# Hybrid attention/S5/MoE layer: hand-placed buffers, early loads, GLU in fp32r, eight-slot q/k store ring

## Chip, core and metric

One core of one Trainium2 chip runs the kernel in one launch, fp32 in and out. The metric is device microseconds of that core.

## What is computed

One layer over 2048 tokens of width 1024. The parts before the residual, cut to what matters:

```python
h = rmsnorm(x, norm_attn)
q, k, v, u = split(h @ w_in)                      # 4 x 512 columns
# differential attention: 4 heads, two causal softmax maps each, ALiBi
a = softmax(q1 k1^T + bias) - lam * softmax(q2 k2^T + bias);  o = a @ v     # then RMSNorm
# S5: 32 groups of 16 channels, each drives a 64-dim complex diagonal state
y = gelu(Re(C states) + D u)
y = y * sigmoid(y @ w_glu + b_glu);  ssm = rmsnorm(y, ssm_norm)
x = x + concat([attn, ssm]) @ w_out
x = x + hier_moe(rmsnorm(x))                      # 32 experts, top 2 of one group
return rmsnorm(x, norm_final)
```

## The kernel before

Every stage is a function with a block of its own: each engine has its instruction list written out by hand, with semaphores between them. A stage ends with a clearing of its semaphores and a barrier of all engines, so nothing of the next stage starts before the last engine of this one is done, the waits for its DMA stores included. Buffers of a stage are allocated at its start and freed at its end.

**norm_project_prepare** (from line 116). Tile by tile of 128 tokens, it normalizes x, transposes it into two fp32r parts (`ht`, hi and lo), and multiplies by w_in in three products (hi hi, lo hi, hi lo). 32 units give v and u. The transposed parts are also stored in `hT_d`. From 225 us on 32 further units, numbered P1 = 32 to 63, give q and k by columns: unit n is a head's 128 columns of q or k for a block of 512 tokens, 8 blocks k of 3 matmuls. Their slices come back from `hT_d` into a ring of 12. ACT writes the hi part of a unit (`hi_out`, L371), DVE the lo part (`lo_out`, L453), ACT's queue stores both (`parts_store`, L379) from `ev`, which has four slots, so two pairs. Before `hi_out` writes a pair it waits until the store of the unit two before has landed. In the same time DVE makes the S5 parameters of eight batches of four groups (`matrices_w`, `matrices_q`, `levels`), two with the tiles, six with the q/k units: `matrices_w(b)` follows lo_out of unit `w_at_unit(b)`, four units apart. PE transposes its result two units later (`batch`, L702, L707). POOL stores q, w and the tables of each batch to DRAM. SP loads u back as `U` and, when all is done, stores the taps.

**s5_groups** (from 774). 16 pairs of groups. SP first loads w, tables (cos, sin), the taps as a Toeplitz block `M`, which DVE has cleared before, and q for the first four groups, then the rest. Per pair: ACT regroups U, PE transposes (L912), ACT copies (`u_group`, L898), PE makes the inputs (L927), DVE turns and adds them (L861 to L864) and scans twice (L871), POOL turns back (L843, L845), PE makes the outputs (L946 to L948), ACT does the GELU into U. States of pair p+2 are queued on PE behind the outputs of pair p.

**s5_gate** (from 962). PE transposes U by 16 columns of 4 blocks, and ACT copies each from PSUM into `yT` (L996), writing every eighth element, 32 bytes apart. Then 16 units n (t = n // 4 a block of 512 tokens, oc = n % 4) of 4 fp32 matmuls (L1052), which run as 8 passes; ACT takes the sigmoid (L1003), DVE the product (L1016), its square (L1020) and the scaled result (L1021). For each t PE adds up the squares of 4 channel blocks and 128 tokens with one-column products (L1043); 16 of them in the program are 32 in the trace. SP stores `ssmT` for each t. At the end DVE and ACT make the root and the reciprocal, `srs`.

**attention** (from 1060). 64 units u (4 heads, 16 row tiles). SP loads q and k of block 0, then five small parameters, v, then blocks 1 to 3. POOL and DVE make the ALiBi ramp (L1148, L1156, L1150). DVE runs score(0), `lam()` (27 tiny steps), score(1), and so on; scores need q, k and the ramp. `out_projection` and the expert stage follow.

## Time and profile before

| | us |
|---|---|
| median of 3 runs | 2337.03 (2335.39 to 2339.47) |
| the profiled execution | 2335.25 |
| its span in the profile | 2333.7 |
| PE busy | 2061.0 (88%) |
| DVE busy | 1365.5 (59%) |
| ACT busy | 1070.4 (46%) |
| POOL busy | 517.3 (22%) |

The profile is one execution. Times in it count from the start of the span. Matmuls are pipelined, so PE can be shown busy while it is slowed by its clock; the granted clock of a stretch is a share of 2.4 GHz, and it has two levels, 2.4 and 1.2 GHz. A releaser is what ended an engine's idle time.

### The profile page before, as it was taken

The page shows a single profiled execution, that of the slowest core. Times are in us where ns is not written, and L with a number is a line of the kernel's source. Part 1 is how long each engine was busy: PE and PEld are TensorE (multiplying, and loading weights), DVE is VectorE, ACT ScalarE, POOL GpSimd, SP SyncE. Part 2 cuts the span into 40 slices and gives each one's busy share as a digit, 9 for nine tenths or more (in the row PEclk, how much of TensorE's full clock was granted, in tenths as well). Part 3 has the DMA queues.
Part 4 walks back from the last instruction along what each step waited for, and adds up shares of the span by engine and source line. Part 5 has one row for each costly group of instructions (what it writes and reads, how often), then busy time and mean ns, then how long its engine had stood idle before and what let it go on. Part 6 is the DMA issues. An engine that isn't in the chain of part 4 may idle for free. (4 is left out here: it accounts for less than half of the span.)

```text
span 2333.7 us, 32329 instructions
## 1 busy us (share of the span) xinstructions
PE 2061.0 (88%) x10318; PEld 1695.1 (73%) x10319; DVE 1365.5 (59%) x2364; ACT 1070.4 (46%) x1580; POOL 517.3 (22%) x631
## 2 busy tenths in 40 slices
PE   6999999698969889897999569999999999999980
PEld 5888777585558677775888358888888888888860
DVE  4674567262357778684444677476658856354544
ACT  3332111134147777774222336475557756454443
POOL 2000011041000000000000025454445644344440
PEclk9999999799879999998999679999999999999995
DMA  8676865650183331203443459698869979576737
GB/s 250 206 233 209 295 234 197 181 199 20 64 206 82 75 91 37 64 1 116 139 141 122 163 221 322 215 340 313 275 231 356 394 245 358 164 261 185 264 82 305
DMA packets 170682, 458.38 MB, mean 196 GB/s; under 512 B 20497, under 2 KB 69729, under 8 KB 144993
## 3 DMA queue, kind: packets, MB, share of 16 engines
q1 hardware_dynamic: 123616, 285.43, 35.8%
q0 software_dynamic: 30848, 138.24, 19.4%
q10 hardware_dynamic: 16128, 33.56, 4.1%
q8 instruction: 51, 0.84, 0.2%
q14 instruction: 39, 0.31, 0.0%
HBM read 342.08 MB, written 115.10 MB: 196 GB/s over the span
## 5 line engine op out<-in xcount | busy, mean ns | idle before, releaser
L1950 DVE TENSOR_TENSOR w_down_lo<-w_down_raw,w_down_hi 128x2048 fp32r<-128x2048 f32 x64 | 144.1, 2289 | 123.2 <-ACT w_down_hi L1887 123.2
L1182 DVE CUSTOM_DVE_ANT_0 scores<-c_bank,alibi 128x512 f32<-128x512 f32 (+3 forms) x320 | 176.3, 606 | 39.2 <-PE c_bank L1295 39.1
L1321 PE MATMUL c_bank<-v_head,map_T 128*128 128x128 f32 x1088 | 150.8, 284 | 32.3 <-ACT map_T L1237 31.0
L1321 PEld LDWEIGHTS c_bank<-v_head,map_T 128*128 128x128 f32 x1088 | 134.0, 194 | 44.6 <-ACT map_T L1237 44.0
L2034 PE MATMUL m_bank<-w_down_hi,hidden_T_hi 128*128 128x512 f32 x392 | 159.7, 407 | 6.8 <-DVE w_down_lo L1950 6.8
L1950 DVE TENSOR_TENSOR w_gate_lo<-w_gate_raw,w_gate_hi 128x2048 fp32r<-128x2048 f32 x63 | 141.6, 2288 | 35.2 <-ACT w_gate_hi L1887 34.1
L1228 ACT ACTIVATE scores<-scores,neg_max 128x128 f32<-128x128 f32 (+15 forms) x128 | 153.5, 1199 | 17.6 <-DVE neg_max L1186 17.6
L2013 PE MATMUL m_bank<-w_gate_hi,rows_T_hi 128*128 128x512 f32 x392 | 156.2, 399 | 4.0 <-issue 2.6
L2013 PE MATMUL m_bank<-w_up_hi,rows_T_hi 128*128 128x512 f32 x392 | 159.0, 406 | 0.0
L2035 PE MATMUL m_bank<-w_down_lo,hidden_T_hi 128*128 128x512 f32 x392 | 155.9, 398 | 0.0
L2014 PE MATMUL m_bank<-w_gate_lo,rows_T_hi 128*128 128x512 f32 x392 | 155.8, 398 | 0.0
L2015 PE MATMUL m_bank<-w_gate_hi,rows_T_lo 128*128 128x512 f32 x392 | 155.7, 397 | 0.0
L1950 DVE TENSOR_TENSOR w_up_lo<-w_up_raw,w_up_hi 128x2048 fp32r<-128x2048 f32 x64 | 146.1, 2286 | 16.3 <-ACT w_up_hi L1887 16.3
L2015 PE MATMUL m_bank<-w_up_hi,rows_T_lo 128*128 128x512 f32 x392 | 154.8, 395 | 0.0
L2014 PE MATMUL m_bank<-w_up_lo,rows_T_hi 128*128 128x512 f32 x392 | 154.8, 395 | 0.0
L1294 PE MATMUL c_bank<-k_hi,q_parts 128*128 128x512 f32 (+3 forms) x320 | 125.9, 398 | 23.6 <-DMA k_lo<-kT_d 14.0
L1606 POOL IOTA count_i<- 128x128 int32 x1 | 0.2, 235 | 656.5 <-POOLq L63 656.5
L1887 ACT ACTIVATE w_up_hi<-w_up_raw 128x2048 fp32r<-128x2048 f32 x62 | 118.6, 1914 | 0.0
L1887 ACT ACTIVATE w_down_hi<-w_down_raw 128x2048 fp32r<-128x2048 f32 x62 | 115.5, 1906 | 6.4 <-DMA w_down_raw<-in_w_down_dram 6.4
L1891 ACT ACTIVATE rows_T_hi<-m_bank 128x512 fp32r<-128x512 f32 x100 | 54.5, 596 | 138.9 <-PE m_bank L2006 138.9
L1295 PE MATMUL c_bank<-k_lo,q_parts 128*128 128x512 f32 (+3 forms) x320 | 116.1, 369 | 0.0
L1902 ACT ACTIVATE rows_out<-m_bank,slot_gate 128x512 f32<-128x512 f32 x98 | 67.5, 688 | 105.9 <-PE m_bank L2039 105.9
(400 smaller groups left out, 5154.0 us busy)
## 6 DMA issues: line engine op xcount, KB each, us to landing
w_gate_raw<-in_w_gate_dram SPq DMA_DIRECT2D x64, 1024.0 KB, 8.2
w_up_raw<-in_w_up_dram SPq DMA_DIRECT2D x64, 1024.0 KB, 8.0
w_down_raw<-in_w_down_dram POOLq DMA_DIRECT2D x64, 1024.0 KB, 8.0
hT_d<-hT_parts SPq DMA_DIRECT2D x32, 512.0 KB, 4.8
hT_parts<-hT_d SPq DMA_DIRECT2D x32, 512.0 KB, 8.3
u_tok<-in_x_dram SPq DMA_DIRECT2D x16, 512.0 KB, 5.0
qT_d<-proj_out ACTq DMA_DIRECT2D x32, 256.0 KB, 3.3
kT_d<-proj_out ACTq DMA_DIRECT2D x32, 256.0 KB, 3.3
```

Of the source, the lines that this page charges most:

```text
L1182: dve.tensor_tensor_reduce(S[:, s, m, c * BANK:c * BANK + w], bank[2 * (n % 2) + m][:, 0:w], ramp[:, x0:x0 + w], SLOPES[h], -BIG, ALU.add, ...
L1228: act.activation(S[:, s, m, 0:L], S[:, s, m, 0:L], ACT.Exp, bias=nm[:, s, m:m + 1], accum_out=rs[:, s, m:m + 1]).then_inc(exped, 1)
L1294: pe.matmul(out, qt, kh[:, ks, m, 0:w].bitcast(F32R), start=True, stop=False)
L1295: pe.matmul(out, qt, kl[:, ks, m, 0:w].bitcast(F32R), start=False, stop=True).then_inc(qk_done, 1)
L1321: last = pe.matmul(bank[6 + u % 2][:, 0:VD], aT[:, n % 2, b * P:(b + 1) * P], v[:, h % 2, kt], start=kt == 0, stop=kt == u % NT)
L1887: act.activation(whi[w][:, halves[i]], raw[w][:, halves[i]], ACT.Copy).then_inc(hi_done[w], 1)
L1950: dve.tensor_tensor(wlo[w][:, halves[i]], raw[w][:, halves[i]], whi[w][:, halves[i]], ALU.subtract).then_inc(lo_done[w], 1)
L2013: pe.matmul(to[:], xh[:, k], whi[w][:, c], start=k == 0, stop=False)
L2014: pe.matmul(to[:], xh[:, k], wlo[w][:, c], start=False, stop=False)
L2015: last = pe.matmul(to[:], xl[:, k], whi[w][:, c], start=False, stop=k == KT - 1)
L2034: pe.matmul(DN[h][:], hh[:, k], whi[2][:, part(k)], start=k == 0, stop=False)
L2035: pe.matmul(DN[h][:], hh[:, k], wlo[2][:, part(k)], start=False, stop=False)
```

## The change

All buffers that live across the four stages get fixed places in the core's memory (`Placed`, `Shared`), so that buffers of the next stage can be filled while a stage still runs.

- Input stage: the q/k parts go to `qk_out` with eight slots, so a write waits for the store of the unit four before; the last waits for these stores move to the next but one stage. PE's and ACT's work on a parameter batch comes one unit later. SP issues all first loads of S5 (w, tables, taps, q, then the second half of the batch) from unit P1 + 28 on; DVE clears the taps behind unit P1 + 25. `ht` and `hT_d` get another layout.
- S5: SP loads only batches 1 to 3 and w_glu; ACT and DVE split w_glu into two fp32r parts (before pair 6's and within pair 8's work).
- Gate: transposes are taken by DVE (five of eight) or ACT (three of eight) and split into hi and lo. Eight columns come before the first unit, eight between units 0 to 3. The GLU is three fp32r products. Squares are added on DVE first, so a group of sums is 4 matmuls. SP loads q and k of attention's first block, POOL makes the ramp alone. `ssmT` has two slots. Root and reciprocal of `srs` move to the out-projection.
- Attention: k and v have other places; the first q/k loads and the ramp are gone.

The core of the diff:

```diff
-        hi_slot = lambda n: 2 * (n % 2)
-        lo_slot = lambda n: 2 * (n % 2) + 1
+        hi_slot = lambda n: 2 * ((n - P1 + 2) % 4)
+        lo_slot = lambda n: hi_slot(n) + 1
...
-        batch_at_unit = {w_at_unit(b) + 2: b for b in range(WITH_TILE, NHB)}
+        batch_at_unit = {w_at_unit(b) + 3: b for b in range(WITH_TILE, NHB)}
...
+                first, later = slice(0, HB), slice(HB, GB)
+                sp.wait_ge(proj_done, P1 + 28)
+                sp.wait_ge(w12_stored, 64)
+                for r, name in enumerate(("w1", "w2")):
+                    sp.dma_start(shared.mats[:, 0, 0, r, first], d[name][0][:, first]).then_inc(shared.w_first, 16)
+                sp.wait_ge(table_stored, 64)
+                for r, name in enumerate(("cos", "sin")):
+                    sp.dma_start(shared.tables[:, 0, r, first], d[name][0][:, first]).then_inc(shared.t_first, 16)
+                sp.wait_ge(taps_stored, 16 * CH)
+                sp.wait_ge(m_zero, 1)
+                for i in range(CH):
+                    sp.dma_start(shared.taps[i * GC:(i + 1) * GC, i:, :], d["taps"][0:CH - i].rearrange("t q g c -> q t (g c)")
+                                 ).then_inc(shared.taps_in, 16)
+                sp.wait_ge(q_stored, 64)
...
                 sp.wait_ge(u_back, 32)
-                sp.wait_ge(taps_stored, 16 * CH)
...
                 def hi_out(n):
                     h = (n - P1) % 4
                     act.wait_ge(proj_done, n + 1)
-                    for s in (hi_slot(n), lo_slot(n)):
-                        act.wait_ge(stored[s], 16 * (8 + (n - P1) // 2))
-                    act.activation(ev[:, hi_slot(n)].bitcast(F32R), bank[4 + n % 3][:], ACT.Copy,
+                    m = n - P1
+                    if m < 2:
+                        for s in (hi_slot(n), lo_slot(n)):
+                            act.wait_ge(stored[s - 4], 16 * 8)
+                    elif m < 4:
+                        act.wait_ge(wlo_done, 7)
+                    else:
+                        for s in (hi_slot(n), lo_slot(n)):
+                            act.wait_ge(shared.qk_stored[s], 16 * (m // 4))
+                    act.activation(qk_out[:, hi_slot(n)].bitcast(F32R), bank[4 + n % 3][:], ACT.Copy,
...
                 parts_store(UNITS - 1)
-                for s in range(4):
-                    act.wait_ge(stored[s], 16 * (8 + 16))
...
+                    if n == P1 + 25:
+                        dve.memset(shared.taps[:], 0.0).then_inc(m_zero, 1)
...
+                        if p == 8 and e == 0:
+                            dve.wait_ge(w_hi_done, 1)
+                            dve.tensor_tensor(shared.w_glu_lo[:], shared.w_glu[:], shared.w_glu_hi[:], ALU.subtract).then_inc(w_lo_done, 1)
...
+        by_act = lambda n: n % 8 in (1, 4, 7)
...
+                for s in range(8):
+                    sp.wait_ge(shared.qk_stored[s], 16 * 8)
...
+                for rows, p in ((top, 0), (low, 1)):
+                    sp.dma_start(shared.q[rows, 0], part_of("qT", p)).then_inc(shared.first_qk_in, 16)
...
+                    if by_act(n):
+                        act.activation(part(yT, n), turned(n), ACT.Copy).then_inc(yT_act, 1)
+                        act.activation(part(yT_hi, n), turned(n), ACT.Copy).then_inc(hi_done, 1)
+                    else:
+                        act.wait_ge(yT_dve, dve_before(n + 1))
+                        act.activation(part(yT_hi, n), part(yT, n), ACT.Copy).then_inc(hi_done, 1)
...
+                for n in range(HALF):
+                    columns(n)
+                    if n >= 2:
+                        columns_lo(n - 2)
+                columns_lo(HALF - 2)
+                columns_lo(HALF - 1)
                 for n in range(16):
...
+                    dve.tensor_tensor(zz[:] if oc else total[:, t % 2], z[:, n % 2], z[:, n % 2], ALU.mult).then_inc(squared, 1)
+                    if t >= 2 and oc == 0:
+                        dve.wait_ge(ssm_st[t % 2], 16)
+                    dve.tensor_scalar(ssmT[:, t % 2, oc], z[:, n % 2], gg[:, oc:oc + 1], None, ALU.mult).then_inc(scaled, 1)
+                    if oc:
+                        dve.wait_ge(squared, n + 1)
+                        dve.tensor_tensor(total[:, t % 2], total[:, t % 2], zz[:], ALU.add).then_inc(added, 1)
+                    if n < 4:
+                        columns(HALF + 2 * n)
+                        columns(HALF + 2 * n + 1)
+                    if 1 <= n < 5:
+                        columns_lo(HALF + 2 * n - 2)
+                        columns_lo(HALF + 2 * n - 1)
...
+                    if n % 8 == 0:
+                        pe.wait_ge(hi_done, HALF * (n // 8 + 1))
+                        pe.wait_ge(lo_done, HALF * (n // 8 + 1))
...
                     for k in range(4):
-                        last = pe.matmul(bank[4 + n % 3][:], wg[:, k, oc * P:(oc + 1) * P], yT[:, k, t * BANK:(t + 1) * BANK],
-                                         start=k == 0, stop=k == 3)
+                        pe.matmul(bank[4 + n % 3][:], wg_hi[:, k, out], yT_hi[:, k, cols], start=k == 0, stop=False)
+                        pe.matmul(bank[4 + n % 3][:], wg_lo[:, k, out], yT_hi[:, k, cols], start=False, stop=False)
+                        last = pe.matmul(bank[4 + n % 3][:], wg_hi[:, k, out], yT_lo[:, k, cols], start=False, stop=k == 3)
                     last.then_inc(glu_done, 1)
+                    if n < 4:
+                        columns(HALF + 2 * n)
+                        columns(HALF + 2 * n + 1)
...
-                load_q(0, 0)
-                load_k(0, 0)
```

## Rows read from the trace of the kernel before

**Rows 1.** The page: PE's busy tenths in 40 slices; a group of part 5

```profile
PE   6999999698969889897999569999999999999980
...
L1950 DVE TENSOR_TENSOR w_gate_lo<-w_gate_raw,w_gate_hi 128x2048 fp32r<-128x2048 f32 x63 | 141.6, 2288 | 35.2 <-ACT w_gate_hi L1887 34.1
```

**Rows 2.** Windows by stage: busy us per engine, granted clock, DMA

```profile
225.00:432.00 207.00, 191.93 (x840) 157.33 (x840) 121.53 (x221) 29.56 (x52) 19.29 (x36) 0.96 0.68 229
432.00:442.00 10.00, 0.00 (x0) 0.00 (x0) 1.22 (x2) 0.73 (x2) 0.14 (x2) 0.60 0.54 157
442.00:548.00 106.00, 85.07 (x576) 77.35 (x577) 56.34 (x81) 29.64 (x65) 40.34 (x32) 0.93 0.50 170
548.00:647.00 99.00, 89.18 (x320) 51.38 (x320) 28.92 (x50) 28.74 (x35) 0.00 (x0) 0.89 0.16 54
647.00:666.00 19.00, 3.35 (x12) 2.85 (x12) 6.17 (x31) 2.16 (x5) 3.74 (x2) 0.59 0.82 179
```

**Rows 3.** Waits, 225 to 442: total us, times, longest us

```profile
ACT proj_out L371 <- DMA qT_d<-proj_out: 25.6, 5, 12.6
```

**Rows 4.** Timeline, 430 to 462: start, us, operation, [idle <- releaser]

```profile
435.03 0.60 ACT L371 ACTIVATE proj_out<-a_bank 128x512 fp32r<-128x512 f32 x1 [3.23 <-DMA kT_d<-proj_out]
...
441.86 1.67 ACT L886 ACTIVATE u_by_group<-u_tok 128x512 f32<-128x512 f32 x3 [6.23 <-PEq L63]
...
453.63 0.69 DVE L861 TENSOR_TENSOR z_in<-b_bank,table_batch 128x512 f32<-128x512 f32 x1 [7.39 <-DMA table_batch<-sin_d]
...
461.11 0.77 PE L946 MATMUL b_bank<-taps_toeplitz,u_group 128*128 128x128 f32 x2 [7.19 <-DMA q_batch<-q_d]
```

**Rows 5.** Timeline of a q/k unit: one product in two neighbouring steps

```profile
419.90 0.39 PE L746 MATMUL a_bank<-hT_parts,w_in_hi 128*128 128x512 f32 x1
...
420.58 0.39 PE L746 MATMUL a_bank<-hT_parts,w_in_hi 128*128 128x512 f32 x1
```

**Rows 6.** Groups of PE, 225 to 442: count, busy us, mean ns, idle

```profile
L707 PE MATMUL a_bank<-C,mat_w 128*128 128x16 f32 x48 | 6.6, 272 | 0.0
L702 PE MATMUL a_bank<-ident,mat_w 128*128 128x128 f32 x24 | 3.9, 284 | 12.4 <-DVE mat_w L572 12.4
```

**Rows 7.** Timeline inside S5: scans without and with POOL; PE waits

```profile
455.68 1.27 DVE L871 TENSOR_TENSOR_SCAN z_state<-r,z_in 128x256 f32<-128x256 f32 x2
...
458.89 2.21 DVE L871 TENSOR_TENSOR_SCAN z_state<-r,z_in 128x256 f32<-128x256 f32 x2
...
474.39 0.46 PE L946 MATMUL b_bank<-taps_toeplitz,u_group 128*128 128x128 f32 x2 [0.80 <-POOL sin_z L845]
...
485.12 0.46 PE L946 MATMUL b_bank<-taps_toeplitz,u_group 128*128 128x128 f32 x2 [0.80 <-POOL sin_z L845]
```

**Rows 8.** Timeline of the gate, and last of a contiguous ACT pair

```profile
548.68 14.96 ACT L996 ACTIVATE yT<-g_bank 128x512 f32<-128x512 f32 x16 [1.50 <-PE g_bank L1034]
...
586.08 3.63 PE L1043 MATMUL g_bank<-ones,squares 128*128 128x1 f32 x32
...
596.73 0.69 ACT L1003 ACTIVATE sigmoid<-g_bank,b_glu 128x512 f32<-128x512 f32 x1 [2.75 <-PE g_bank L1052]
600.16 0.69 ACT L1003 ACTIVATE sigmoid<-g_bank,b_glu 128x512 f32<-128x512 f32 x1 [2.75 <-PE g_bank L1052]
...
619.88 0.69 DVE L1016 TENSOR_TENSOR gated<-yT,sigmoid 128x512 f32<-128x512 f32 x1 [1.62 <-ACT sigmoid L1003]
...
621.22 0.48 DVE L1021 TENSOR_SCALAR ssmT<-gated,ssm_gain 128x512 f32<-128x512 f32 x1
...
1051.85 1.05 ACT L1237 ACTIVATE map_T<-c_bank 128x512 f32<-128x512 f32 x2
```

**Rows 9.** Timeline of DVE at the start of attention: score(0) and score(1)

```profile
660.22 0.29 DVE L1182 CUSTOM_DVE_ANT_0 scores<-c_bank,alibi 128x128 f32<-128x128 f32 x1 [9.98 <-PE c_bank L1295]
...
665.85 0.41 DVE L1182 CUSTOM_DVE_ANT_0 scores<-c_bank,alibi 128x256 f32<-128x256 f32 x1
```

**Rows 10.** DMA issues, 540 to 646: count, KB, median us to landing

```profile
ssmT_d<-ssmT SPq DMA_DIRECT2D x4, 1024.0 KB, 4.4
```

More of the change, by code:

```diff
@@ L45 @@
 BIG = 3.0e38
+KSLOTS = 5
 META_ID = NBLK
@@ L894, in _ @@
                         regroup(p + 2)
+                    if p == 6:
+                        act.wait_ge(w_glu_in, 16)
+                        act.activation(shared.w_glu_hi[:], shared.w_glu[:], ACT.Copy).then_inc(w_hi_done, 1)
                     act.wait_ge(uT, p + 1)
@@ L985, in _ @@
+                for p in range(2):
+                    for rows in (top, low):
+                        sp.dma_start(shared.k[rows, KSLOTS - 1, p], part_of("kT", p)).then_inc(shared.first_qk_in, 16)
                 for t in range(4):
                     sp.wait_ge(scaled, 4 * (t + 1))
-                    cols = slice(t * BANK, (t + 1) * BANK)
-                    sp.dma_start(d["ssmT"][:, :, cols], ssmT[:, :, cols]).then_inc(ssm_st, 16)
-                sp.wait_ge(ssm_st, 64)
+                    sp.dma_start(d["ssmT"][:, :, t * BANK:(t + 1) * BANK], ssmT[:, t % 2]).then_inc(ssm_st[t % 2], 16)
@@ new lines, in _ @@
+                for i in range(2):
+                    sp.wait_ge(ssm_st[i], 32)
+            @block.gpsimd
+            def _(pool):
+                t, ti = ramp[:], ramp[:].bitcast(I32)
+                for s in range(8):
+                    pool.wait_ge(shared.qk_stored[s], 16 * 8)
+                pool.iota(ti, pattern=[[1, SEQ]], base=-(SEQ - P), channel_multiplier=-1).then_inc(ramp_step, 1)
+                pool.wait_ge(ramp_step, 1)
+                pool.tensor_copy(t, ti).then_inc(ramp_step, 1)
+                pool.wait_ge(ramp_step, 2)
+                pool.affine_select(out=t, in_=t, pattern=[[-1, SEQ]], compare_op=ALU.is_ge,
+                                   fill=-BIG, base=SEQ - P, channel_multiplier=1).then_inc(ramp_step, 1)
+                pool.wait_ge(ramp_step, 3)
@@ L991, in _, with columns @@
             @block.scalar
             def _(act):
[L993 to L994 removed]
+                def columns(n):
                     act.wait_ge(yT_psum, n + 1)
[L996 to L998 removed]
+                    if by_act(n):
[4 more added lines that the diff above has]
+                        act.activation(part(yT_hi, n), part(yT, n), ACT.Copy).then_inc(hi_done, 1)
@@ L999, in _ @@
+                act.preload_act_table(ACT.Sigmoid)
+                for n in range(HALF):
+                    columns(n)
+                act.wait_ge(small_in, 32)
                 for n in range(16):
@@ L1035, in _ @@
                     last.then_inc(yT_psum, 1)
-                pe.wait_ge(yT_done, 2 * CH)
-                pe.wait_ge(ld, 48)
                 def sums(t):
-                    pe.wait_ge(squared, 4 * (t + 1))
+                    pe.wait_ge(added, 3 * (t + 1))
                     for i in range(4):
-                        for k in range(4):
-                            last = pe.matmul(bank[7][:, 4 * t + i:4 * t + i + 1], sq[:, t % 2, k, i * P:(i + 1) * P], ones[:, 0:1],
-                                             start=k == 0, stop=k == 3)
+                        last = pe.matmul(bank[7][:, 4 * t + i:4 * t + i + 1], total[:, t % 2, i * P:(i + 1) * P], ones[:, 0:1],
+                                         start=True, stop=True)
                     last.then_inc(sum_done, 1)
+                for n in range(HALF):
+                    columns(n)
                 for n in range(16):
                     t, oc = n // 4, n % 4
+                    cols, out = slice(t * BANK, (t + 1) * BANK), slice(oc * P, (oc + 1) * P)
+                    if n % 8 == 0:
+                        pe.wait_ge(hi_done, HALF * (n // 8 + 1))
+                        pe.wait_ge(lo_done, HALF * (n // 8 + 1))
                     if n >= 3:
@@ L1057, in _, with attention @@
                 sums(3)
-def attention(nc, ident, ones, oT, wo, a, d):
+def attention(nc, ident, ones, shared, oT, wo, a, d):
     UN = HEADS * NT
```

287 lines of the change are left out of this document (168 added, 119 removed).

## The prediction

> **What bounds the kernel now.** Four views, in this order. First the page's slices [rows 1]: TensorE (PE) is 90% busy or more in most of them, so time is won only where its row dips or its clock falls. Second, each engine's busy time cut at the stage borders [rows 2]: 225 to 432 is the q/k part of the input stage, 442 to 548 S5, 548 to 647 the gate, 647 to 666 the start of attention. Third, the waits of the q/k part [rows 3]. Fourth, the timeline at the borders [rows 4, 9] and inside S5 and the gate [rows 7, 8]. PE stands idle for 15 us of 207 in the q/k part, for the whole 10 us between the stages and for most of 19 us at the start of attention. In the gate it is 90% busy, but with work that the change makes cheaper. The 1668 us from 666 on hold nothing that the change touches, but for two tiny operations. The profiled execution took 2335.25 us (span 2333.7); the median of the runs shown is 2337.03, 1.8 more. The sum is made against 2335.25, and 1.8 is added at the end.
>
> **q/k part, 32 units (columns, hi_out, lo_out).** A unit is 24 matmuls, three in 0.68 us [rows 5], so 5.44 us; 32 make 174. The six parameter batches beside them have 24 transposes and 48 small products [rows 6], about 8 us at 0.11 each. So 182 us of work stand in 207. The other 25 are 15 us of idle PE and about 8 us of half clock: the granted clock is 0.96 of full [rows 2], so 16.6 us ran at 1.2 GHz, and half of that is lost. Of the idle time 12.4 us are waits of the mat_w transposes on DVE [rows 6]. They arise so: ACT may not write slot pair n before the store of n-2 has landed (25.6 us of waits on qT_d stores alone, up to 12.6 us [rows 3]); lo_out waits for ACT, matrices_w stands behind lo_out on DVE, and PE wants mat_w before the second unit after. The change doubles the ring (a wait now asks for the store of n-4, 21.8 us of cover instead of 10.9) and puts the batch one unit later. I take 22 of the 25; the bounds are 10 (waits or half clock stay in part) and 25. The new hT_d layout keeps its 512-byte and 2-KB pieces; I cost it at nothing, since PE's only other waits in that stage, 2.7 us, are for DVE, none for a slice. If slices came late, PE would wait at the three block changes, 0 to 5 us each.
>
> **Border to S5.** Now: ACT waits 3.2 us for a store before its last part at 435.03, DVE and a store follow, S5's first operation is at 441.86 [rows 4]. PE has nothing for 10 us [rows 2]. The last waits for stores go (they move to the gate's SP and GpSimd (POOL) queues, when the stores have long landed). Left are ACT 0.6, DVE 0.69, two DMA issues of about 1 us, the barrier about 1.2: 3.6 us. Gain 6.4, bounds 0 to 7. SyncE (SP) must issue 8 tap stores and 20 loads in the 21.8 us of the last four units; the same 20 loads took it 12 us at the start of S5, so there is room unless the queue backs up. DVE's clearing of the taps, 128x4096, at most twice the 2.29 us of a 128x2048 operation [rows 1], goes behind the work of unit 25; PE has two units of cover there.
>
> **Start of S5.** Now DVE waits 7.4 us for the tables and PE 7.2 us for q; the first output product is at 461.11, 19.3 us in [rows 4]. Without DMA waits the chain is: regroup and transpose 1.9, u_group 0.6, eight products at half clock 3.7, DVE 3.2, POOL 2.5, hand-overs 0.4: 12.3. The second pair, now 26.6 us in, comes at about 17.4, behind the first one's products on PE. So everything behind starts 9.2 us sooner; bounds 5 to 11. The next batch, 4 MB, is needed some 25 us in, which is what the stage's mean of 170 GB/s [rows 2] brings in that time. Later pairs are a loop, two pairs in 10.7 us with PE waiting 0.8 us for POOL [rows 7]. The new w_glu subtraction, 128x2048 and 2.29 us [rows 1], stands between an addition and a scan in that loop: minus 2.0 (0 to 2.3). The ACT copy, some 1.9 us, fits into ACT's idle time (30 of 106 us busy [rows 2]).
>
> **Gate.** Now 99.1 us, 548.02 to 647.11. Sixteen strided ACT copies take 14.96 us, 0.935 each; sixteen GLU units of eight passes follow at 3.43 us, and four groups of 32 one-column products, 3.5 us each at full clock [rows 8]. After: a unit is twelve fp32r products at 0.227, 2.72; a group of sums has 8 instructions, 0.9. Only eight columns stand ahead of the first unit, with eleven ACT writes (three columns are written twice): 10.3 us, plus first transpose and last subtraction 3: first unit at 13.4. Then DVE leads. Product, square and scaling take 1.82 [rows 8], with the new addition 2.45 per unit; during units 0 to 4 five copies and eight subtractions come on top. Their strided form isn't in the trace. Lower bound is the contiguous 0.62 and 0.69, upper bound ACT's factor (0.935 against 0.50 a copy [rows 8]), 1.1 and 1.4; I take 0.9 and 0.95, nearer to the plain rows because DVE is the slower engine per element. Laid out in order, DVE reaches the fourth addition 37 us in and the last subtraction 46 us in; unit 8 starts there, eight units at 2.72 with two sums and 2 us of waits end at 71.6. Sigmoid, product, square and scaling make 3, the last ssmT store 4.9 (issue 0.5, landing 4.4 [rows 10]). That store was hidden by the fourth group of sums; now it ends last. With the barrier 80.5 instead of 99.1; less 0.6 for low clock while PE waits for DVE: gain 18, with the bounds 24 and 6.
>
> The Trainium skill (SBUF — State Buffer, "Door 1: The DMA port swizzle") says that consecutive accesses within a 16-byte line are fast and that each crossing to another line pays. The trace agrees for ACT: 0.935 against 0.50 us [rows 8]. The columns are written 32 bytes apart, so by the page DVE's would pay too, as in the first rival.
>
> **Start of attention.** First scores now 13.1 us in, because q/k are waited for; then lam() holds DVE until score(1) at 665.85, 18.7 us in [rows 9]. After: q/k are there and the ramp is made in the gate. Five small loads lead SP and should have landed 5 us in, lam() takes 5.0 (the difference of [rows 9] less score(0)), so score(1) at 10.1: gain 8.6, not 12. v, 1 MB behind them at 179 GB/s [rows 2], lands 9 to 11 us in and is needed at 12.7. Block 1 of q/k makes it 2.7 MB, 18 us in, due at 17.6. That is tight; the bounds are 4 and 9.5. Square root and reciprocal go to the out-projection: minus 0.4.
>
> **Sum.** 22 + 6.4 + 9.2 - 2.0 + 18 + 8.6 - 0.4 = 61.8. 2335.25 - 61.8 + 1.8 = 2275.3, say 2275.
>
> **Rivals.**
> Strided DVE work is dear (18%): copies and subtractions at 1.1 and 1.4 us, ACT's reads as slow. The gate ends 12 us later: 2287 (2284 to 2293). For: 0.935 against 0.50. Against: DVE is slower per element.
> GpSimd blocks DVE (5%): iota, cast and select on POOL lie on the gate's first subtractions. In S5 two scans beside POOL work took 2.21 us instead of 1.27 [rows 7], a delay of 0.9. If each subtraction waited for a whole POOL operation, the first unit would come up to 5 us later: 2280. The skill's page SBUF — State Buffer ("SBUF: two separate sides") has it as an exclusive lock held for the whole instruction, by which it would be these 5 us.
> The early loads or the ring don't help (13%): SP is still issuing when the input stage ends, or the batch waits stay because DVE itself is late. 10 to 25 us of the first three terms are lost: 2285 to 2300.
> More than forecast (7%): strided operations cost what plain ones do and no clock drops: 2258 to 2263.
> Slower (3%): all 26 strided DVE operations of the gate lie on the path. At 3.3 us each they eat all terms (26 x 2.4 = 62); from there on the kernel is slower, at 3.5 us it is 2342. Only the unseen form speaks for it; ACT's factor of 1.9 would give 1.4 us.
> No change (1%): the same at the point between.
> The forecast itself 53%, its own range 2264 to 2284.
>
> **How the numbers follow.** The range leaves out half of the best case, the slower and the no-change case and the tail of the third: 2260 to 2297. A measurement of this kernel can tell about 0.2%, 4.7 us. Faster by more than that 0.96, within it 0.01, slower 0.03.
>
> **What would show it.** In the q/k part: no wait of mat_w transposes on DVE over 1 us, clock 0.99 or more, 32 units in 183 to 190 us. Border 3 to 5 us. S5's first output 11 to 13 us in, with no DMA among its releasers. Gate 75 to 88 us; PE waits for DVE up to unit 8, and the end is the ssmT store. Attention: score(1) 10 us in. Wrong would be: SP issuing after the last q/k matmul; a PE wait on hT slices; strided DVE operations above 1.1 us.

## The result and the profile after

| | before | changed |
|---|---|---|
| median, us | 2336.21 (2332.98 to 2339.47, 4 runs) | 2275.06 (2274.78 to 2278.07, 4 runs) |
| span of the profiled execution | 2333.7 | 2273.2 |

The ratio is 0.9737, with a 95% interval of 0.9717 to 0.9757. The forecast was 2275. The windows by stage of the changed kernel, in the columns of [rows 2]; the stages are the q/k part, the border, S5, the gate and the start of the attention up to score(1):

```profile
core 0: us, PE busy (x) PEld busy (x) DVE busy (x) ACT busy (x) POOL busy (x), PEclk, DMA share, GB/s
220.50:403.00 182.50, 182.50 (x840) 151.71 (x840) 124.74 (x221) 29.55 (x52) 19.35 (x36) 1.00 0.83 273
403.00:406.80 3.80, 0.02 (x1) 0.00 (x0) 1.38 (x2) 0.60 (x1) 0.00 (x0) 0.79 1.06 280
406.80:506.20 99.40, 86.01 (x576) 77.10 (x576) 55.08 (x81) 31.47 (x66) 40.50 (x34) 0.94 0.46 172
506.20:591.60 85.40, 63.57 (x288) 52.26 (x288) 63.14 (x87) 34.52 (x39) 6.29 (x3) 0.85 0.22 68
591.60:603.40 11.80, 3.33 (x12) 2.85 (x12) 4.84 (x30) 2.16 (x5) 0.00 (x0) 0.50 0.61 142
```

Set against [rows 2] the rows tell three things. In the q/k part PE's busy time is the whole window and the clock is full. In the gate PE works 25.6 us less (63.6 of 85.4 against 89.2 of 99.0), but the gate is only 13.7 shorter, since DVE's work has grown from 28.9 to 63.1 us and PE waits for it, with a granted clock of 0.85 over the stage. And in the attention's start PE still has next to nothing to do. The stages one by one, from the first and last instruction of each (gains are taken before rounding):

| stage | before | changed | gain | forecast |
|---|---|---|---|---|
| up to the first q/k unit | 224.98 | 220.47 | 4.5 | 0 |
| q/k part | 206.9 | 182.6 | 24.3 | 22 |
| border | 10.0 | 3.8 | 6.2 | 6.4 |
| S5 | 106.2 | 99.4 | 6.8 | 9.2 - 2.0 |
| gate | 99.1 | 85.4 | 13.7 | 18 |
| attention, to score(1) | 18.7 | 11.8 | 7.0 | 8.6 |
| all behind it | 1667.8 | 1669.8 | -2.0 | -0.4 |
| span | 2333.7 | 2273.2 | 60.5 | 61.8 |

Where the stages changed, four timelines of the changed kernel: ACT's last two parts of the q/k part and S5's first operation; SP's last early load; PE's first output product of S5; DVE at the start of the attention.

```profile
402.38 0.60 ACT L449 ACTIVATE qk_out<-a_bank 128x512 fp32r<-128x512 f32 x1 [9.60 <-PE a_bank L824]
403.38 0.60 ACT L449 ACTIVATE qk_out<-a_bank 128x512 fp32r<-128x512 f32 x1 [0.40 <-PE a_bank L824]
406.87 1.67 ACT L950 ACTIVATE u_by_group<-u_tok 128x512 f32<-128x512 f32 x3 [2.90 <-PEq L65]
...
400.40 0.93 SPq L337 DMA_DIRECT2D mat_batch<-q_d  x2
...
419.27 0.46 PE L1013 MATMUL b_bank<-taps_toeplitz,u_group 128*128 128x128 f32 x2
...
592.34 0.29 DVE L1318 CUSTOM_DVE_ANT_0 scores<-c_bank,alibi 128x128 f32<-128x128 f32 x1 [3.41 <-PE c_bank L1432]
598.52 0.23 DVE L1299 TENSOR_TENSOR o_head<-o_head 128x64 f32<-128x64 f32 x1 [5.27 <-DMA subln<-in_attn_subln_dram]
603.31 0.15 DVE L1304 TENSOR_SCALAR subln<-subln 128x1 f32<-128x1 f32 x1
603.38 0.41 DVE L1318 CUSTOM_DVE_ANT_0 scores<-c_bank,alibi 128x256 f32<-128x256 f32 x1
```

ACT is released by PE alone where a store released it in [rows 4]. The last early load is issued 2.6 us before PE ends. S5's first output comes 12.4 us in (19.3 before, [rows 4]). In the attention score(0) is 0.7 us in, DVE then waits 5.27 us for lambda's loads and computes for 4.9, and only then comes score(1).

### The profile page after: what moved, and what is told of

It is laid out like the page before. It is cut to its first block and busy times, and to the rows that moved or that the text cites. A ratio compares the mean times of both kernels' runs of the same rounds, so it can differ in the third digit from the quotient of the medians.

```text
span 2273.2 us, 32351 instructions
## 1 busy us (share of the span) xinstructions
PE 2026.7 (89%) x10286; PEld 1689.8 (74%) x10287; DVE 1400.1 (62%) x2402; ACT 1078.5 (47%) x1586; POOL 522.9 (23%) x632
## 3 DMA queue, kind: packets, MB, share of 16 engines
q0 software_dynamic: 30848, 138.24, 19.8%
## 5 line engine op out<-in xcount | busy, mean ns | idle before, releaser
L1431 PE MATMUL c_bank<-k_parts,q_parts 128*128 128x512 f32 (+3 forms) x320 | 125.8, 398 | 12.6 <-DVE max_part L1318 6.8
L2044 ACT ACTIVATE rows_out<-m_bank,slot_gate 128x512 f32<-128x512 f32 x98 | 67.5, 689 | 106.2 <-PE m_bank L2181 103.6
L1432 PE MATMUL c_bank<-k_parts,q_parts 128*128 128x512 f32 (+3 forms) x320 | 116.2, 370 | 0.0
```

The costliest lines, as they stand in the source:

```text
L1431: pe.matmul(out, qt, k_of(4 * h + c, 0)[:, m, 0:w].bitcast(F32R), start=True, stop=False)
L1432: pe.matmul(out, qt, k_of(4 * h + c, 1)[:, m, 0:w].bitcast(F32R), start=False, stop=True).then_inc(qk_done, 1)
```

## The experiments

All but e9 start from the changed kernel. Their stage times are read as above, from the profiled execution of each; ratios are to the kernel before, run beside each group.

**e1: two slot pairs again.**

```diff
-        hi_slot = lambda n: 2 * ((n - P1 + 2) % 4)
+        hi_slot = lambda n: 4 + 2 * ((n - P1) % 2)
...
-                    elif m < 4:
-                        act.wait_ge(wlo_done, 7)
...
-                            act.wait_ge(shared.qk_stored[s], 16 * (m // 4))
+                            act.wait_ge(shared.qk_stored[s], 16 * (m // 2))
...
```

> The changed kernel with the q/k store ring back at two slot pairs; the parameter batch stays one unit later. Theory (the ring gives most of the 24.3 us won in the q/k part, because ACT no longer waits for stores): ACT's waits on q/k stores come back at 10 us or more, PE waits for DVE on mat_w again, the part takes 195 to 200 us instead of 182.6, and the whole is 12 to 18 us slower than the changed kernel, 2287 to 2293. Rival (the later batch alone does it, ACT may wait as it likes): the waits of ACT come back but PE's don't, the part stays at 182 to 185 us, the whole within 3 us of 2275.

**e2: the parameter batch back at its unit.**

```diff
-        batch_at_unit = {w_at_unit(b) + 3: b for b in range(WITH_TILE, NHB)}
+        batch_at_unit = {w_at_unit(b) + 2: b for b in range(WITH_TILE, NHB)}
```

> The changed kernel with the parameter batch back at the second unit after its inputs; the eight-slot ring stays. Theory: with the ring lo_out is on time and matrices_w comes out on DVE early enough, so PE waits for mat_w 0 to 0.6 us a batch (six batches, 0 to 4 us); the part takes 182 to 187 us, the whole 2275 to 2279. Rival (the batch's place is what removed the 12.4 us of waits): mat_w waits of about 2 us a batch are back, some clock is lost with them, the part takes 195 us or more, the whole 2287 or more.

**e3: both.** The edits of e1 and e2.

> Both undone: two slot pairs and the early batch, the rest of the changed kernel as it is (the new layout of the stored state and the early loads too). Theory: ring and batch are all of the gain in the part, so it is back at 205 to 208 us, the granted clock there at 0.96, the whole 22 to 25 us slower than the changed kernel, 2297 to 2300. Rival (the new layout of the store between the stages has a share): the part takes 195 us or less.

| | q/k part | half clock in it | border | ratio to before |
|---|---|---|---|---|
| changed | 182.6 | 0.0 | 3.8 | 0.9737 (0.9717 to 0.9757) |
| e1, ring of two | 190.8 | 3.4 | 16.7 | 0.9832 (0.9803 to 0.9861) |
| e2, early batch | 196.6 | 10.2 | 3.8 | 0.9806 (0.9774 to 0.9838) |
| e3, both | 205.1 | 17.1 | 14.1 | 0.9890 (0.9861 to 0.9919) |

Medians: 2299.76, 2295.12 and 2313.69 us. The theories of e1 and e2 missed. Of e1 neither the 195 to 200 us of the theory nor the rival's 182 to 185 came; of e2 the rival's 195 us or more did. The ring alone carries 8.3 us of the part, the batch's place 14.0, and they add up (22.3 against 22.6 for both). And the ring carries 12.9 us at the border, where nothing was expected. e3's part and clock came as its theory had them, and its rival falls: the new layout of the stored state has no share, since e9, with the old one, took 205.3 us for the part. But e3's median lies 14 us above the expected 2300; 10.2 us of that stand at the border and 3.7 in S5. Waits of PE and ACT, in the columns of [rows 3], first of e1, then of e2, then of e3; PE's from 220 us on to the end of the part, ACT's to the end of the stage:

```profile
PE a_bank L820 <- DVE qk_out L527: 3.4, 3, 2.9
PE a_bank L778 <- DVE mat_w L646: 1.9, 2, 1.0
ACT qk_out L447 <- DMA qT_d<-qk_out: 76.8, 16, 13.0
ACT qk_out L447 <- DMA kT_d<-qk_out: 59.6, 11, 10.5
```

```profile
PE a_bank L780 <- DVE mat_w L648: 8.6, 3, 2.9
```

```profile
PE a_bank L778 <- DVE mat_w L646: 10.5, 4, 2.9
```

In e1 ACT waits 136 us for stores, 117.5 of them within the part, and PE only 5.3 us for DVE. In e2 ACT waits for no store, and yet PE waits 8.6 us for mat_w. With both undone it is 10.5. So 1.9 us of the mat_w waits come from the stores, and 8.6 don't. What makes mat_w late is the order and length of DVE's own work, here in e2:

```profile
278.90 0.69 DVE L529 SCALAR_TENSOR_TENSOR qk_out<-a_bank,qk_out 128x512 fp32r<-128x512 f32 x1 [4.46 <-ACT qk_out L449]
279.51 0.18 DVE L668 COPY table<-table_first 128x64 f32<-128x64 f32 x1
...
289.64 0.69 DVE L590 TENSOR_TENSOR table<-table,table_tmp 128x512 f32<-128x512 f32 x1
290.37 0.15 DVE L673 COPY table_tmp<-table 128x1 f32<-128x1 f32 x1
290.56 0.69 DVE L529 SCALAR_TENSOR_TENSOR qk_out<-a_bank,qk_out 128x512 fp32r<-128x512 f32 x1
291.17 0.68 DVE L646 TENSOR_TENSOR mat_w<-powers_rev,b1bar 128x512 f32<-128x512 f32 x1
292.61 0.69 DVE L648 TENSOR_TENSOR mat_w<-mat_w,table_tmp 128x512 f32<-128x512 f32 x1
```

From 278.90 on DVE has no idle time: 10 us of table building, with two of the units' sums among them, stand ahead of mat_w. Just before, DVE stood idle for 4.46 us, because the sum of the next unit comes first in its program and had to wait for ACT. One unit more until PE wants mat_w is 5.4 us of cover.

**e12: ring of two, and the first S5 loads at the start of S5.** The edits of e1 and of e4 (below).

> The changed kernel with two slot pairs in the q/k ring and the first S5 loads issued at the start of S5. With the ring alone undone the q/k part took 190.8 us and the border 16.6; with the loads alone undone 182.6 and 3.8. Theory (the early S5 loads, 5.6 MB of them beside the last units' stores, make the stores slow, and only the eight-slot ring lets ACT go on past them): without the early loads ACT hardly waits in the last six units, the part takes 184 to 188 us and the border 4 to 8; the two changes are worth much less apart than together. Rival (the stores are slow in the last units by themselves, whatever is loaded): the border stays at 12 us or more. Either way S5 takes about 110 us as with the loads alone undone; the whole 2290 to 2297 by the theory, 2300 or more by the rival.

The part took 191.5 us (like e1: more than the theory's 184 to 188), the border 6.7, which is the theory's and not the rival's, S5 111.8; median 2299.26, ratio 0.9830 (0.9799 to 0.9860), above the theory's 2297 and just under the rival's 2300. ACT's last timeline rows of e1, then of e12:

```profile
415.73 0.60 ACT L447 ACTIVATE qk_out<-a_bank 128x512 fp32r<-128x512 f32 x1 [10.51 <-DMA kT_d<-qk_out]
424.71 0.60 ACT L447 ACTIVATE qk_out<-a_bank 128x512 fp32r<-128x512 f32 x1 [8.38 <-DMA kT_d<-qk_out]
```

```profile
411.96 0.60 ACT L426 ACTIVATE qk_out<-a_bank 128x512 fp32r<-128x512 f32 x1 [7.25 <-PE a_bank L801]
415.79 0.60 ACT L426 ACTIVATE qk_out<-a_bank 128x512 fp32r<-128x512 f32 x1 [3.23 <-DMA kT_d<-qk_out]
```

With the early loads beside them the last k stores hold ACT for 18.9 us, without them for 3.2. So of the ring's 12.9 us at the border 10 are due only because of the early loads: without the ring they would give at the start of S5 (11.1 us, e4) hardly more than they take at the end of the input stage. Without the early loads the ring gives 2.8 us at the border (6.7 to 3.8), which leaves 3.3 (10.0 to 6.7) for the rest of the change there. No run undoes that alone; the moved store waits are the likely part.

**e4: the first S5 loads at the start of S5.** Twelve of them and the eight tap loads go from SP's program of the input stage to that of S5.

```diff
             @block.sync
-                for r, name in enumerate(("w1", "w2")):
-                    sp.dma_start(shared.mats[:, 0, 0, r, first], d[name][0][:, first]).then_inc(shared.w_first, 16)
...
             @block.sync
+                for r, name in enumerate(("w1", "w2")):
+                    sp.dma_start(shared.mats[:, 0, 0, r, first], d[name][0][:, first]).then_inc(shared.w_first, 16)
...
```

> The changed kernel with the first S5 loads (matrices, tables, taps, q) issued at the start of S5 again, as before the change; the clearing of the taps stays early and the store waits stay moved. Theory: the first output product comes 19 us into S5 instead of 12.4, PE waits for q and DVE for the tables, and every later pair moves with it: S5 takes 6 to 9 us more (105 to 108), the border stays at 3 to 4 us since it hangs on the moved store waits, the whole is 2281 to 2284. Rival 1 (the border too hangs on the loads): it is back at 6 us or more. Rival 2 (S5's pair loop makes up for a late start, since another engine leads it): S5 takes under 102 us.

The first output is 20.5 us in, the border 3.9 (rival 1 falls), S5 110.4 (rival 2 falls). That is 11.1 us more than with the early loads, above the 6 to 9 expected: half clock in S5 rose from 12.0 to 19.8 us, which is 3.9 of it. Median 2288.80, above the expected 2281 to 2284, ratio 0.9788 (0.9757 to 0.9818). PE's waits at the start of S5 in e4, none of which is in the changed kernel:

```profile
PE b_bank L1008 <- DMA mat_batch<-q_d: 7.1, 1, 7.1
PE b_bank L989 <- DMA mat_batch<-w_d: 4.2, 1, 4.2
```

**e5: the first q/k loads at the start of the attention.** The six q/k loads go from SP's program of the gate to that of the attention, ahead of lambda's five.

```diff
-                    sp.dma_start(shared.q[rows, 0], part_of("qT", p)).then_inc(shared.first_qk_in, 16)
...
+                    sp.dma_start(shared.q[rows, 0], part_of("qT", p)).then_inc(shared.first_qk_in, 16)
...
```

> The changed kernel with the first six q/k loads issued at the start of the attention again, ahead of the five small loads for lambda; the ramp stays in the gate. Theory (at the start of the attention the early q/k loads are the gain, as the forecast has it): the first scores wait for the landing, lambda's loads come behind, and score(1) is 17 to 19 us in instead of 11.8; the whole is 5 to 7 us slower than the changed kernel, 2280 to 2282. Rival (the ramp's move is what counts, and lambda hides the rest): score(1) at 13 us or less, the whole within 2 us.

score(1) is 18.8 us in, as before the change; median 2282.05, ratio 0.9776 (0.9754 to 0.9798). The theory holds: the gain of this stage is that of the early loads.

**The gate: e6, the ramp after the last subtraction.**

```diff
+                pool.wait_ge(lo_done, 2 * CH)
```

> The changed kernel with GpSimd's ramp for the attention (index, cast, select) made only after the last of the gate's subtractions. Theory: in the changed kernel one subtraction took 1.91 us beside a GpSimd operation where the others take 1.07 to 1.10, so GpSimd costs DVE 0.8 us ahead of the first unit and nothing later; the first unit comes at 15.2 to 15.5 us into the gate instead of 16.1, and the gate is 0.5 to 1 us shorter (84.4 to 84.9). Rival (each of the early subtractions waits for a whole GpSimd operation): 3 us or more sooner, gate 82.5 or less. Rival 2 (ACT and PE are late by themselves, the half clock above all): nothing moves, 85.4.

The first unit came 14.5 us in instead of 16.1, 1.6 sooner (between the expectations), but the gate took 89.6 us, 4.3 more, which none of them has. It ran once, in 2275.78 us, so only the trace can be read. DVE and POOL in the changed kernel at the start of the gate, then in e6 in the middle of it:

```profile
508.49 1.90 POOL L1085 CAST alibi<-alibi 128x2048 f32<-128x2048 int32 x1
510.54 2.55 POOL L1087 TENSOR_SCALAR_AFFINE_SELECT alibi<-alibi 128x2048 f32<-128x2048 f32 x1
509.40 1.91 DVE L1128 TENSOR_TENSOR yT_lo<-yT,yT_hi 128x512 fp32r<-128x512 f32 x1 [0.41 <-ACT yT_hi L1100]
511.24 1.11 DVE L1120 COPY yT<-g_bank 128x512 f32<-128x512 f32 x1
512.18 2.86 DVE L1128 TENSOR_TENSOR yT_lo<-yT,yT_hi 128x512 fp32r<-128x512 f32 x2
```

```profile
557.41 1.86 POOL L1084 IOTA alibi<- 128x2048 int32 x1 [54.42 <-DVE yT_lo L1129]
559.33 1.97 POOL L1086 CAST alibi<-alibi 128x2048 f32<-128x2048 int32 x1
561.44 2.15 POOL L1088 TENSOR_SCALAR_AFFINE_SELECT alibi<-alibi 128x2048 f32<-128x2048 f32 x1 [0.15 <-POOL alibi L1086]
557.86 0.69 DVE L1150 TENSOR_TENSOR gated_sq<-gated 128x512 f32<-128x512 f32 x1
558.47 1.08 DVE L1153 TENSOR_SCALAR ssmT<-gated,ssm_gain 128x512 f32<-128x512 f32 x1
559.46 2.37 DVE L1156 TENSOR_TENSOR sum_of_squares<-sum_of_squares,gated_sq 128x512 f32<-128x512 f32 x1
561.76 2.37 DVE L1144 TENSOR_TENSOR gated<-yT,sigmoid 128x512 f32<-128x512 f32 x1
564.17 0.69 DVE L1150 TENSOR_TENSOR gated_sq<-gated 128x512 f32<-128x512 f32 x1
```

The addition of 559.46 ends 0.53 us behind the cast and the product of 561.76 0.54 behind the select: each waited until the POOL operation had ended, then took its own time. The copy of 511.24 (from g_bank) ran beside the select at 1.11, and the square of 557.86 beside the index at 0.69. The Trainium skill (SBUF — State Buffer, "SBUF: two separate sides") says that a DVE operation with two inputs in SBUF and a GpSimd operation that reads SBUF exclude each other for a whole instruction, and that a DVE operation in a two-port mode and any GpSimd operation do too. By the first half the index, which reads nothing, doesn't block an operation with two inputs; the trace agrees in the addition, the product, the copy and the square. The scaling of 558.47 has one tensor as its input. It took 1.08 us where the other fifteen of e6 took 0.48, and ended 0.28 behind the index, so it did wait for the index. That fits the second half, but no run here shows in which mode the scaling runs.

In the changed kernel such waiting costs two subtractions 0.8 us each, the 1.6 us of e6. In e6 it costs two operations of the busiest stretch 1.7 each and the scaling 0.6, 4.0 us together; PE waits 5.2 us at one group of sums and the clock is at half from 566.7 to 573.5 us.

**e7: the columns written side by side.** Tokens inside each half stand in another order; the work is the same, but the output isn't the layer's.

```diff
-        part = lambda t, n: t[:].rearrange("p k (h m j) -> p k h m j", h=2, j=CH)[:, :, n // CH, :, n % CH]
+        part = lambda t, n: t[:].rearrange("p k (h j m) -> p k h j m", h=2, j=CH)[:, :, n // CH, n % CH]
```

> The changed kernel with the gate's columns written side by side instead of 32 bytes apart; the tokens inside each half are in another order there, so the output of the S5 branch isn't the reference's, and the number and size of all operations stay. It prices the strided form of DVE's copies and subtractions (1.07 to 1.12 us) and ACT's copies. Theory: they take 0.62 to 0.69 and about 0.5 to 0.6 us; DVE gets ahead by 21 operations of some 0.4 us, 8 to 9 us, before unit 8; the first unit comes at 12 to 14 us in, unit 8 at 43 to 46 instead of 51.8, and the gate takes 77 to 80 us instead of 85.4, the whole 2267 to 2270. Rival (PE, with its half clock, or the additions and scans of the first units lead, not the strided form): the gate takes 83 us or more, though the operations are shorter.

The gate took 73.3 us, 12.1 less and below the 77 expected; the first unit is 12.0 us in. Groups of the gate, in the columns of [rows 6], of the changed kernel and of e7:

```profile
L1128 DVE TENSOR_TENSOR yT_lo<-yT,yT_hi 128x512 fp32r<-128x512 f32 x16 | 19.0, 1242 | 0.8 <-ACT yT_hi L1100 0.4 <-ACT yT_hi L1097 0.4
L1100 ACT ACTIVATE yT_hi<-yT 128x512 fp32r<-128x512 f32 x10 | 11.8, 1187 | 14.0 <-DVE yT L1120 13.7 <-PE g_bank L1175 0.3
L1120 DVE COPY yT<-g_bank 128x512 f32<-128x512 f32 x10 | 10.7, 1108 | 7.8 <-PE g_bank L1175 7.8
```

```profile
L1128 DVE TENSOR_TENSOR yT_lo<-yT,yT_hi 128x512 fp32r<-128x512 f32 x16 | 13.1, 855 | 0.0
L1120 DVE COPY yT<-g_bank 128x512 f32<-128x512 f32 x10 | 6.7, 682 | 8.0 <-PE g_bank L1175 8.0
L1100 ACT ACTIVATE yT_hi<-yT 128x512 fp32r<-128x512 f32 x10 | 6.3, 632 | 14.8 <-DVE yT L1120 14.8
```

The strided form costs a copy 1.11 us instead of 0.68 and a subtraction 1.06 to 1.4 instead of 0.68, both where no POOL operation is beside it. DVE's busy time falls by 9.0 us (63.1 to 54.2), and since PE waits less, half clock in the gate falls from 26.0 to 9.8 us, which is 8.1 us more. These are two readings of one cause and partly the same time, so they add up to more than 12.1. The whole, 2245.11 us at a ratio of 0.9596, can't be compared: with another order of tokens the last stage makes 384 instead of 392 products of each kind and everything behind score(1) is 20.9 us shorter.

**e8: the GLU as plain fp32 products.** No upper and lower parts of the state or of w_glu. The first copies of the columns go half to ACT and half to DVE.

```diff
-                        pe.matmul(bank[4 + n % 3][:], wg_hi[:, k, out], yT_hi[:, k, cols], start=k == 0, stop=False)
-                        pe.matmul(bank[4 + n % 3][:], wg_lo[:, k, out], yT_hi[:, k, cols], start=False, stop=False)
-                        last = pe.matmul(bank[4 + n % 3][:], wg_hi[:, k, out], yT_lo[:, k, cols], start=False, stop=k == 3)
+                        last = pe.matmul(bank[4 + n % 3][:], wg[:, k, out], yT[:, k, cols], start=k == 0, stop=k == 3)
...
-        by_act = lambda n: n % 8 in (1, 4, 7)
+        by_act = lambda n: n % 2 == 1
...
```

> The changed kernel with the GLU as plain fp32 products (four passes), so no upper and lower part of the state or of w_glu: no subtraction on DVE, no second write on ACT, the columns in turn by DVE and ACT. All else of the change stays. A unit costs PE 3.43 us instead of 2.72. Theory (DVE leads the changed gate, and its lateness also costs clock: 25.9 us of half clock there; the three products give back less than their preparation costs): the first unit comes 6 to 8 us in, sixteen units take 55 us, the sums 3.6, the tail 8: 72 to 76 us instead of 85.4, with half clock under 15 us; S5 is 2 us shorter (97.4) without the w_glu subtraction; the whole is 11 to 14 us faster than the changed kernel, 2261 to 2264. Rival (PE leads, so each unit costs 0.7 us more): the gate takes 90 us or more, the whole is 2280 or more. Rival 2 (the strided copies of the second half still hold the units up): the gate takes 79 to 84 us.

**e9: the kernel before, with the squares of a group added on DVE.** Sums of 4 products instead of 16 per column group.

```diff
+                    if oc:
...
+                        dve.tensor_tensor(sq[:, t % 2, 0], sq[:, t % 2, 0], sq[:, 0, 3], ALU.add).then_inc(added, 1)
...
-                        for k in range(4):
-                            last = pe.matmul(bank[7][:, 4 * t + i:4 * t + i + 1], sq[:, t % 2, k, i * P:(i + 1) * P], ones[:, 0:1],
-                                             start=k == 0, stop=k == 3)
+                        last = pe.matmul(bank[7][:, 4 * t + i:4 * t + i + 1], sq[:, t % 2, 0, i * P:(i + 1) * P], ones[:, 0:1],
+                                         start=True, stop=True)
```

> The kernel before, with one part of the change alone: the squares of a group are added on DVE, so that a group of sums is 8 instructions' work (4 one-column products) instead of 32. Theory: each of the four groups falls from 3.5 us on PE to about 0.9, 10.4 us together, and DVE has room for 12 additions of 0.69 us beside the four fp32 passes; but the last ssmT store (4.9 us) is no longer hidden by the last group, so 3 to 4 us come back: the gate takes 92 to 94 us instead of 99.1, the whole is 5 to 8 us faster than before (ratio 0.9966 to 0.998). Rival (the additions make DVE late for each group, PE waits 2 us or more a group): the gate takes 96 us or more, the ratio is 0.999 or more. It also shows whether the start of the q/k part, which is 4.5 us later in the kernel before than in the changed one (224.98 against 220.47) though no edit explains that, is at 225 again (then it belongs to the change) or moves from run to run with the granted clock.

The gate's windows, in the columns of [rows 2], of e8 and of e9:

```profile
510.80:585.60 74.80, 67.30 (x224) 35.47 (x224) 43.85 (x69) 20.72 (x25) 5.64 (x3) 0.97 0.26 78
```

```profile
543.90:628.20 84.30, 72.30 (x224) 36.53 (x224) 36.12 (x62) 28.73 (x35) 0.00 (x0) 0.93 0.18 63
```

In e8 the gate took 74.7 us, as expected, though PE is busy 3.7 us longer than in the changed kernel; the first unit is 5.3 us in, half clock 5.1 us. Median 2266.80, ratio 0.9716 (0.9700 to 0.9732): the interval overlaps that of the changed kernel, so by the runs alone the two aren't told apart for sure, while the stage's 10.7 us are plain in the trace. The median missed the expected 2264 by 3 us. Why isn't shown; the profiled execution, the fastest of the five at 2265.64, reached the first q/k unit at 224.2, 3.8 us later than the changed kernel. S5 took 100.3 us (100.4 in e11), not less than 99.4; but versions with the changed kernel's S5 code, itself among them, take 99.1 to 99.4 us, or 102.9 to 103.1 with PE waiting longer for POOL (13.6 us in e7 against 9.7 in the changed kernel). Only if e8's is of the second kind, as its 12.9 us of half clock suggest (12.7 to 13.1 there, 10.2 to 12.0 in the first), is it 2.6 shorter. That stays open.

In e9 the gate fell from 99.1 to 84.3 us (92 to 94 expected) and the ratio is 0.9899 (0.9870 to 0.9928), median 2315.76. The ratio is worth 23.6 us, where 5 to 8 were expected and the gate gives 14.8; the rest isn't explained by the edit. The two profiled executions differ by 19.2 us, of which 4.5 lie ahead of the q/k part, the difference that is taken up at the end of the next section. The first two groups of sums took PE 0.95 us each instead of 3.63, the last, at half clock in both, 1.87 instead of 6.82. Half clock fell from 22.0 to 11.6 us. This small edit alone gives as much as the whole new gate (85.4). So the three fp32r products, worth 11.4 us of PE by the forecast, give nothing here: what they save on PE they cost on DVE, and without them the new gate is 10.7 us shorter still (e8).

**e10: lambda in the gate, and e11: e8 and e10 together.** The five loads go to SP's program of the gate, lam() to DVE's, ahead of its first wait for a sigmoid.

```diff
+                for n, name in enumerate(("lambda_q1", "lambda_k1", "lambda_q2", "lambda_k2")):
+                    sp.dma_start(shared.lam_in_rows[:, n], a[name].to_broadcast([P, HD])).then_inc(lam_in, 16)
...
+                lam()
...
-                    if n == 0:
-                        lam()
...
```

> The changed kernel with lambda's five small loads at the start of the gate and lambda's arithmetic on DVE there, in the 5.7 us in which DVE waits for the first sigmoid. Theory (at the start of the attention only lambda holds DVE and so score(1)): score(1) comes 2.5 to 3.5 us in instead of 11.8; then v (landed 10.5 us in) and the next block of q/k hold PE, so that about 5 us are left of the 9; the gate stays within 1 us of 85.4; the whole is 4 to 6 us faster, 2269 to 2271. Rival 1 (the loads of v and q/k bind the stage just behind): score(1) is early but the whole moves by less than 2 us. Rival 2 (lambda's arithmetic doesn't fit into DVE's wait, since DVE leads the gate): the gate is 3 us or more longer and eats the gain.

> The GLU as plain fp32 products and lambda in the gate, together, on the changed kernel: a version meant to beat both kernels. Theory: the two gains add, since they lie in stages one behind the other: gate 72 to 77 us, score(1) 2.5 to 3.5 us in, the whole 2256 to 2260 (a ratio to before of 0.966 to 0.968). Rival (DVE in the fp32 gate has no wait of 5 us left for lambda, and the first unit's DVE work comes late): the gate is 3 to 5 us longer than with fp32 alone, the whole 2260 to 2264.

PE's waits in the attention's start, of e10:

```profile
PE c_bank L1459 <- DMA v_head<-v_d: 4.9, 1, 4.9
PE c_bank L1432 <- DMA k_parts<-kT_d: 1.4, 1, 1.4
```

score(1) came 1.7 us in with both. In e10 the gate took 85.5 us: rival 2 falls, lambda is hidden in DVE's wait. PE's first product with v is 8.9 us in instead of 14.3, so 5.4 us are left there. Yet the median is 2274.00 (2269 to 2271 expected) and the ratio 0.9739 (0.9722 to 0.9757), that of the changed kernel, with single runs from 2268.5 to 2276.3. The profiled execution is the fastest of the five: its span is 6.3 us shorter than the changed kernel's, with as much half clock behind score(1) (174.5 and 174.8 us). So there the gain was kept, against rival 1. What took it back in the three slower runs isn't settled. e11's gate took 74.7 us, its median is 2262.78, its ratio 0.9691 (0.9675 to 0.9707). That interval lies below the changed kernel's: e11 beats both kernels. It missed the expected 2260 by 3 us. Its profiled execution is the slowest of the five, at 2268.07: everything behind score(1) took 11.8 us more than in the changed kernel, with 193.4 us at half clock against 174.8.

## Why the prediction was right, point by point

**q/k part (22 forecast, 24.3 measured): the size was right, the reason half wrong.** The step that failed is "They arise so: ACT may not write slot pair n before the store of n-2 has landed", by which the ring would remove the mat_w waits. e2 has no wait for a store and 8.6 us of mat_w waits; e1 has 117.5 us of waits for stores in the part and 1.9. Most of the waits arise from 10 us of table work ahead of mat_w on DVE, and the batch's later place is worth 14.0 us, the ring 8.3. The reading error was to join two wait lists of [rows 3, 6] because they lay in one stretch. That full clock would follow when the waits go was right: 17.1 us at half clock became none.

**Border (6.4 and 6.2): right,** with a part that the forecast costed at nothing. "SP ... so there is room unless the queue backs up" looked only at issuing; the loads' transfers beside the stores take 10 us at the border where the ring is small (e1 against e12). The ring hid a cost that the forecast hadn't seen.

**S5 (9.2 - 2.0 and 6.8): right in kind, in size partly by chance.** The first output came 12.4 us in, 12.3 forecast. e4 prices the early loads at 11.1 us, at the upper bound of 11. The w_glu subtraction took 2.29 us, as in [rows 1], but that it lengthens S5 by 2.0 no run shows (e8 left it open). And the stage varies from execution to execution: 99.1 to 103.1 us with the changed code, 106.2 and 108.3 with the old one (the kernel before and e9). One pair of them can give 3 to 9 us.

**Gate (18 and 13.7): right in kind, two terms mis-sized.** "I take 0.9 and 0.95, nearer to the plain rows because DVE is the slower engine per element" failed: the copies took 1.11, the subtractions 1.06 to 1.4, which is the first rival's price for copies, so the first unit came at 16.1 us (13.4 forecast), the fourth addition ended 43 us in (37) and the last subtraction 52 us in (46). Strided DVE operations above 1.1 us were the forecast's own sign of being wrong, and they are there. The rival's 12 us were too many, since it put all subtractions at 1.4; 4.9 of them came. The second is the clock: 0.6 us were taken, but 26.0 us of the changed gate ran at half clock (22.0 of the old one), and the first unit alone took 5.1 us there instead of 2.72. Forecast and rivals had the same shape right: DVE leads, the last store ends the stage (issued at 586.23, next stage at 591.61). What neither saw is that the GLU's products then bring nothing (e8, e9).

**GpSimd blocks DVE (rival, up to 5 us): it does, for 1.6 us** in the changed kernel.

**Attention (8.6 and 7.0): the mis-sized term is "should have landed 5 us in":** lambda's loads had all landed 6.9 us in, and score(1) came at 11.8 instead of 10.1.

**Not forecast: 4.5 us ahead of the q/k part.** They aren't the change: the kernel of e9, which has none of it there, reached the first unit at 220.43, and e8, which has all of it, at 224.23. Clock is most of it: the two late ones, e8 and the kernel before, have 10.2 us at half clock up to there, the changed kernel 3.4, which is 3.4 of the 4.5 us. All others have 3.4 or 6.8 and reach the unit at 220.3 to 221.7. Without them the profiled execution would have gained 56.0 us, not 60.5, against 61.8 forecast: that the totals agree so well is in part luck.

## What to carry to other kernels

A wait that disappears with an edit isn't proof that the edit's mechanism made it: undo the parts one at a time before giving one the credit. When work is moved to another engine to make TensorE's shorter, lay out that engine's time with the real access pattern first; here plain fp32 products with nothing to prepare beat three cheap ones by 10.7 us in the gate. Loads made early compete with the stores of the stage that they are moved into, so ask what buffer depth those stores have.

## What the runs showed of the hardware that was not expected

Writing fp32 columns 32 bytes apart costs DVE nearly as much as ACT: 1.11 against 0.68 us a copy of 128x512, a subtraction 1.1 to 1.4 against 0.68, an ACT copy 1.19 against 0.63 (changed kernel against e7). A DVE operation on two SBUF tensors waits until a GpSimd cast or select has ended (0.69 us became 2.37, e6), but not for the index (0.69), and a DVE copy from PSUM doesn't wait (1.11 beside the select). A scaling of one tensor did wait for the index, once (0.48 us became 1.08, e6).

The granted clock made waits of TensorE dearer than their length: in the changed gate it fell to half within the wait of 8.2 us ahead of the first unit, and the unit took 5.1 us instead of 2.72. It also fell where TensorE was busy: in the kernel before it was at half for 3.4 us just behind the second group of 32 one-column products, for 6.9 from within the third and for 8.3 from within the last, though PE had no wait ahead of the second and third. With 8 products a group (e9) that was so only at the last, for 4.8 us. The gate got 14.8 us shorter, where four groups at full clock would give 10.7.
